# Sampled keys turned by VectorE in 32x32 squares instead of by TensorE, and their scores in four row groups

## What is computed

```python
past_k = cache_k[l][page_table].reshape(DB, past, N_HEADS, HEAD_DIM)   # DB = 8, past = 512
k_all  = jnp.concatenate([past_k, k], axis=1)
z      = jnp.einsum('bqhd,bkhd->bhqk', q, k_all) * (HEAD_DIM ** -0.5) + sb_bias
# sigmoids of -z are multiplied up from the last key to the first, their steps weight v_all
```

## Time and profile before

| | |
|---|---|
| median of 3 runs | 1088.38 us |
| profiled execution, its own time | 1088.52 us |
| its span, first to last instruction | 1086.7 us |
| TensorE busy | 1042.7 us (96%) |
| VectorE busy | 541.6 us (50%) |
| ScalarE busy | 308.5 us (28%) |
| mean granted TensorE clock | 0.986 of full speed |

### The profile page before, as it was taken

The page is one execution under the profiler, slowest core; times in us unless marked ns, Lnnn a source line. Parts: engine busy times, 40 slices in busy tenths (PEclk is TensorE's granted clock), DMA queues, the critical chain, the costliest instruction groups (busy, mean ns, idle before and its releaser), DMA issues.

```text
span 1086.7 us, 29226 instructions
## 1 busy us (share of the span) xinstructions
PE 1042.7 (96%) x12774; PEld 822.1 (76%) x12774; DVE 541.6 (50%) x1052; ACT 308.5 (28%) x592; POOL 176.2 (16%) x160
## 2 busy tenths in 40 slices
PE   7999999999999989999999999999999889989996
PEld 7999999966666549899876898656898556656565
DVE  6326654379875553344743554555445534343431
ACT  6323332266775552222411111111110110101011
POOL 1001300599300000100011111111111111111102
PEclk9999999999999999999999999999999998989998
DMA  7356785000106467767899999999999999999994
GB/s 246 108 166 202 228 277 152 1 14 2 40 27 214 149 233 263 235 227 274 319 368 385 384 387 386 387 381 375 385 377 388 377 392 397 382 388 395 381 390 110
DMA packets 85817, 293.19 MB, mean 270 GB/s; under 512 B 13426, under 2 KB 44850, under 8 KB 60070
## 3 DMA queue, kind: packets, MB, share of 16 engines
q1 hardware_dynamic: 78277, 273.30, 67.3%
q0 software_dynamic: 7280, 17.58, 6.8%
q10 hardware_dynamic: 128, 0.39, 0.1%
HBM read 272.98 MB, written 42.87 MB: 291 GB/s over the span
## 4 chain that ended last, share of the span: by engine, by line
PE 79%; DMA 13%; DVE 3%; SPq 2%; ACT 1%; issue 1%; POOL 0%; ACTq 0%; POOLq 0%
PE bank L2830 24%; PE bank L2375 12%; DMA w_all<-in_w_up 12%; PE bank L2612 8%; PE bank L2418 4%; PE bank L2847 4%; PE bank L2851 3%; PE bank L2584 3%; PE bank L2547 3%; PE bank L2456 2%; PE bank L2855 2%; SPq L1042 2%; PE bank L2479 1%; PE bank L2696 1%; DVE keep L1887 1%; PE bank L2371 1%
## 5 line engine op out<-in xcount | busy, mean ns | idle before, releaser
L2830 PE MATMUL bank<-w_all,xeT 128*32 128x256 f32 x6144 | 349.1, 385 | 19.2 <-DMA w_all<-in_w_up 15.6
L2830 PEld LDWEIGHTS bank<-w_all,xeT 128*32 128x32 f32 x6144 | 253.8, 111 | 107.4 <-issue 27.2
L2202 DVE STREAM_TRANSPOSE xeT<-xg 32x256 f32<-32x256 f32 x360 | 156.5, 435 | 102.7 <-DMA xg<-n_scr,tab 97.6
L2847 PE MATMUL bank<-w_all,hT 128*32 128x256 f32 x744 | 165.6, 379 | 0.0
L2851 PE MATMUL bank<-w_all,hT 128*32 128x512 f32 x744 | 129.0, 592 | 0.0
L1887 DVE TENSOR_TENSOR_SCAN keep<-keep,unseen 128x1024 f32<-128x1024 f32 (+7 forms) x64 | 94.8, 1514 | 37.2 <-ACT keep L1439 37.1
L2375 PE MATMUL bank<-w_hi,xh 128*128 128x256 f32 x376 | 108.1, 287 | 0.0
L2375 PE MATMUL bank<-w_hi,xl 128*128 128x256 f32 x376 | 105.5, 281 | 0.0
L2375 PE MATMUL bank<-w_lo,xh 128*128 128x256 f32 x376 | 105.5, 280 | 0.0
L2847 PEld LDWEIGHTS bank<-w_all,hT 128*32 128x32 f32 x744 | 81.8, 110 | 30.4
L1681 ACT ACTIVATE sgl<-bank 128x384 f32<-128x384 f32 x32 | 15.7, 491 | 304.0 <-PE bank L2830 304.0
(11 more groups left out here) (307 smaller groups left out, 1492.9 us busy)
## 6 DMA issues: line engine op xcount, KB each, us to landing
w_all<-in_w_down SPq DMA_DIRECT2D x64, 1024.0 KB, 30.0
w_all<-in_w_gate SPq DMA_DIRECT2D x64, 1024.0 KB, 29.4
w_all<-in_w_up SPq DMA_DIRECT2D x64, 1024.0 KB, 32.7
k_scr<-in_cache_k SPq DMA_DIRECT2D x32, 256.0 KB, 3.5
v_scr<-in_cache_v SPq DMA_DIRECT2D x32, 256.0 KB, 3.4
pgk<-k_scr SPq DMA_DIRECT2D x32, 256.0 KB, 4.0
w_raw<-in_w_in SPq DMA_DIRECT2D x7, 1024.0 KB, 7.1
pgv<-v_scr SPq DMA_DIRECT2D x4, 1024.0 KB, 5.9
```

Source lines behind the costliest of these rows:

```text
L2202: last = dve.transpose(xeT[i][rows_of(s), :, rows_of(g)], lane[:, :, s, :])
L2830: lasts = [pe.matmul(pair_ps(i)[rows_of(q), g, :, :], xeT[i][:, k, rows_of(g)], pair_of(b, i, k, q), start=(k == 0 and g != 1), stop=(k == ...
L2847: return pe.matmul(y_right_ps(g), hT[:, ft, rows_of(g)], w[ft // 2][:, ft % 2, DA:D], start=first and g != 1, stop=ends, skip_group_check= ...
```

## The change

`pgk` gets another layout: partition 32b + r holds row r of each of the 16 chunks (of 32 keys) of sequence b, so that one DMA fills 32 partitions. VectorE turns a set with four instructions of 128x512, in squares of 32x32, from SBUF to SBUF, two ahead of each of the two scans of the turn (`turn_keys`). After that, partition 32b + r of a chunk's square s holds column 32s + r of sequence b: the contraction over 128 columns lies in four slices of 32, all four of one sequence on the same 32 partitions. `past_scores` therefore has 16 matmuls for a set in place of 4: for each slice q, four matmuls with contraction over 32 partitions, sequence b in row group b and column group b. Their weights are windows of `qz_squares`, which VectorE clears and fills in turn 16 (`spread_squares`: one memset of 128x1056 and 16 copies), after the last pooling product, in whose place in SBUF it lies.

Gone are `past_keys` of TensorE and `copy_keys` of ScalarE and VectorE. SyncE waits for `s_hms` (keys turned) where it waited for `s_t`.

```diff
@@ places
+    SQUARE = PAGE // SQ
+    CHUNKS, SPLIT = PAST // SQUARE, P // SQUARE
+    pgk = [place(f"pgk{i}", [P, CHUNKS, P], F32, at_k[i])[0] for i in range(2)]
+    qz_squares, at = place("qz_squares", [P, HP * SPLIT * (DB // SQ) + 1, SQUARE], F32, at_m + 512 + 2 * slot)
@@ SyncE, load_keys(k)
-                    sp.wait_ge(s_t, turned("keys", k - 2, SQ - 1))
+                    sp.wait_ge(s_hms, keys_turned(k - 2))
                 for b in range(SQ):
-                    src = k_scr[SQ * g + b].rearrange("j p f -> p j f")[:, :, P * hp:P * hp + P]
-                    sp.dma_start(pgk[k % 2][:, b, :, :], src).then_inc(s_kld[k % 2], 16)
+                    src = k_scr[SQ * g + b].rearrange("j (c r) f -> r (j c) f", r=SQUARE)[:, :, P * hp:P * hp + P]
+                    sp.dma_start(pgk[k % 2][SQUARE * b:SQUARE * (b + 1), :, :], src).then_inc(s_kld[k % 2], 16)
@@ ScalarE and VectorE: copy_keys removed
@@ VectorE
+            def spread_squares():
+                dve.wait_ge(s_pm, NUS)
+                chain.link(dve.memset(qz_squares[:, :, :], 0.0))
+                out = qz_squares[:, 0:HP * SPLIT * NSG, :].rearrange("p (h s g) e -> p h s g e", s=SPLIT, g=NSG)
+                new = qT[:, :, TP:T].rearrange("p h (g b j) -> p h g b j", g=NSG, b=SQ)
+                for b in range(SQ):
+                    for q in range(SPLIT):
+                        last = dve.tensor_copy(out[SQUARE * b:SQUARE * (b + 1), :, q, :, SQUARE - DS:SQUARE],
+                                               new[SQUARE * q:SQUARE * (q + 1), :, :, b, :])
...
+            def turn_keys(k, half):
+                if half == 0:
+                    dve.wait_ge(s_kld[k % 2], 16 * SQ * (k // 2 + 1))
+                    dve.wait_ge(s_za, scored(NARROW_FROM - 1))
+                    dve.wait_ge(s_zb, scored(NARROW_FROM - 1))
+                    if k >= 2:
+                        dve.wait_ge(s_zp, SQ * (k - 1))
+                for q in range(2 * half, 2 * half + 2):
+                    last = dve.transpose(kTs[k % 2][:, q, :], pgk[k % 2][:, SPLIT * q:SPLIT * (q + 1), :].rearrange("p c f -> p (c f)"))
...
+                if i == NARROW_FROM - 1:
+                    spread_squares()
@@ TensorE: past_keys removed; past_scores(k)
-                for b in range(SQ):
-                    rows = slice(32 * b, 32 * b + 32)
-                    pe.matmul(z_past_ps[rows, :], qz[:, hp, SQ * g + b, :], kTs[k % 2][:, b, :],
-                              start=(hp == 0), stop=(hp == HP - 1)).then_inc(s_zp, 1)
+                keys = kTs[k % 2].rearrange("p q (c s r) -> p s q c r", s=SPLIT, r=SQUARE)
+                for q in range(SPLIT):
+                    n, h = (hp * SPLIT + q) * NSG + g, 2 * hp + q * SQUARE // HD
+                    lo = SQUARE * n + SQUARE - DS - DS * h
+                    for b in range(SQ):
+                        rows = slice(SQUARE * b, SQUARE * (b + 1))
+                        last = pe.matmul(z_past_ps[rows, :], qz_squares[rows, :, :].rearrange("p n e -> p (n e)")[:, lo:lo + SQUARE],
+                                         keys[rows, q], start=(hp == 0 and q == 0), stop=(hp == HP - 1 and q == SPLIT - 1))
+                        if q == SPLIT - 1:
+                            last.then_inc(s_zp, 1)
```

More of the change, by code:

```diff
@@ L454, in hybrid_step @@
     for i in range(NU + 2):
-        for k in range(NKEY):
-            if i == key_turn(k):
-                ring += [(("keys", k, j), "act" if j % 2 == 0 else "dve") for j in range(2)]
         for g in range(NSG):
@@ L462, in hybrid_step @@
                 ring += [(("smp", g), "dve")]
-        for k in range(NKEY):
-            if i == key_turn(k):
-                ring += [(("keys", k, j), "act" if j % 2 == 0 else "dve") for j in range(2, SQ)]
         if 1 <= i <= NU:
@@ L987, in _ @@
                 load_keys(k)
-            sp.wait_ge(s_t, turned("keys", NKEY - 2, SQ - 1))
+            sp.wait_ge(s_hms, keys_turned(NKEY - 2))
             load_values(2)
@@ L996, in _ @@
             load_values(5)
-            sp.wait_ge(s_t, turned("keys", NKEY - 1, SQ - 1))
+            sp.wait_ge(s_hms, keys_turned(NKEY - 1))
             def load_w_out(n):
@@ L1479, in keep_past @@
                                scale=-HD ** -0.5).then_inc(s_sgp, 1)
[L1481 to L1487, removed]
             def copy_sample_weights(g):
@@ L1572, in _ @@
                     keep_head(i, 0)
-                for k in range(NKEY):
-                    if i == key_turn(k):
-                        copy_keys(k, 0)
                 if i == 1:
@@ L1902, in sample_weights @@
                 dve.tensor_tensor(smp_w[:, :], smp_keep[:, 1:NKS + 1], smp_keep[:, 0:NKS], ALU.subtract).then_inc(s_am, 1)
-            def copy_keys(k, j):
-                n = ring_at["keys", k, j]
-                dve.wait_ge(s_t, turned("keys", k, j))
-                if k >= 2:
-                    dve.wait_ge(s_zp, SQ * (k - 1))
-                dve.tensor_copy(kTs[k % 2][:, j, :], bank[:, 4 + n % 2, :]).then_inc(s_td, 1)
+            def spread_squares():
[7 more added lines that the diff above has]
+                                               new[SQUARE * q:SQUARE * (q + 1), :, :, b, :])
+                        if (b, q) != (SQ - 1, SPLIT - 1):
+                            chain.done(last)
+                last.then_inc(s_qz, 1)
+            def turn_keys(k, half):
[7 more added lines that the diff above has]
+                    last = dve.transpose(kTs[k % 2][:, q, :], pgk[k % 2][:, SPLIT * q:SPLIT * (q + 1), :].rearrange("p c f -> p (c f)"))
+                    if q < CHUNKS // SPLIT - 1:
+                        chain.done(last)
+                if half == 1:
+                    last.then_inc(s_hms, 1)
             def lo_sample(g):
@@ L2470, in scores @@
                                 last.then_inc((s_za, s_zb)[a], 1)
-            def past_keys(k, samples):
-                if 0 in samples:
-                    pe.wait_ge(s_kld[k % 2], 16 * SQ * (k // 2 + 1))
-                for b in samples:
-                    n = ring_at["keys", k, b]
-                    free_bank(n)
-                    for j in range(NPG):
-                        last = pe.transpose(t_ps(n)[:, j, :], pgk[k % 2][:, b, j, :], ident[:, :])
-                    last.then_inc(s_t, 1)
             def new_scores(g):
@@ L2667, in _ @@
                     sum_values(i - 2, 0)
-                for k in range(NKEY):
-                    if i == key_turn(k):
-                        past_keys(k, (2, 3))
                 if 2 <= i < NU + 2:
```

22 lines of the change are left out of this document (10 added, 12 removed).

## The result

The changed kernel takes 1097.09 us, the median of four runs (1093.77 to 1099.6), where the kernel before took 1088.52 in four runs beside it: a ratio of 1.0076, 95% interval 1.0054 to 1.0098, which is 8.3 us more (5.9 to 10.7). Four more runs later gave 1.0083 (1.0066 to 1.0101). The forecast was 1093.2, so slower is right and 3.9 us are missing from the sum. The measured time lies above the forecast's own range (1090.8 to 1096) and inside the wide one (1088.8 to 1101.5).

A forecast was written before the change was run, and what follows sets the result against it. TensorE's issue was taken to bound the turns. Its own sum +2.6, recovered waits -1.1 and the start +3.3 gave +4.8 us on 1088.52: 1093.2 us, own range 1090.8 to 1096, wide range 1088.8 to 1101.5.

The forecast's parts named there:

- rival 2: Samples' scores: row groups side by side overlap only in part, 4.4 us a set, total 1099.8 us; 12%.
- TensorE's own sum: TensorE over eight sets: scores +20.5, page turns gone -16.7, sums merged -1.2, together +2.6 us.
- 3 (13.6): Samples' scores: one bank, one row group at a time, 13.6 us a set, total about 1174 us; 3%.
- rival 5: Samples' scores: the four groups of a set overlap in pairs, total 1079.6 us; 6%.
- waits of the ring: Turns 23 and 24: TensorE's waits for ScalarE's copies from the two-bank ring go, -1.1 us.
- rival 4: VectorE becomes the bound: a 128x512 turn takes 1.4 us instead of 0.72, total 1104 us; 4%.
- the DMA paragraph: Page loads: about 6 of 6.66 us needed, covered; a possible VectorE wait of about 1 us, mostly in spare time.
- The start: Turns 16 and 17: `spread_squares` delays VectorE's unit-16 scans and TensorE waits; together +3.3 us, between +0.5 and +4.5.
- the 0.5 for the first scores of the samples: After turn 17: VectorE's first key turns end at 335.6, TensorE wants them at 335.1, +0.5 us.
- Rival 1: The start is hidden, unit-16 scans hardly wait: 1090.5 us or less; 18%.
- That is +2.8 us: Turn 17: TensorE waits for both unit-16 scans and ends at about 333.0 instead of 330.2.
- What stays until the end: After attention: the weight stream moves by the same amount, so time gained or lost in the turns is kept.

The follow-up runs named there:

- the repeat: The changed kernel again, unaltered, against the kernel before: median 1097.6 us, ratio 1.0083; its profiled execution took 1093.79 us.
- e_warm: The changed kernel with eleven identity matmuls in turn 17 that keep TensorE from idling: 1092.6 us, ratio 1.0035.
- e_spread_in_before: The kernel before with `spread_squares` (one memset, sixteen copies) added in turn 16, read by nobody: 1092.28 us, ratio 1.0023.
- e_early_filled: The changed kernel with `qz_squares` filled in turns 11 to 15, plus eight identity matmuls in three later TensorE waits: 1090.63 us, ratio 1.0013.
- e_turned_scratch: The changed kernel with key pages laid in DRAM scratch in 32-column slices, scores again four matmuls over 128 partitions, no `qz_squares`: 1078.02 us, ratio 0.9901.
- the early squares: The changed kernel with `qz_squares` moved, cleared in turn 11 and filled in turns 12 to 15, run in two series: 1092.72 and 1093.28 us.
- e_before_filled: The kernel before with eight identity matmuls in its own waits at 392, 394 and 406 us: 1088.97 us, ratio 1.0004.
- e_one_group: The changed kernel with only the first of four contraction slices in the past keys' scores, 4 matmuls a set: 1086.48 us, ratio 0.9967.

## Why the prediction was right, and where it was short

The sign and the core of the sum are right by their mechanism. That the time lies in the stated range is partly luck: 1097.09 is above the forecast's own range of 1090.8 to 1096, and the part of the wide range that takes it in was there for rival 2 (1099.8), which the trace refutes.

*TensorE's own sum, +2.6, held.* A set's scores took 3.57 us (forecast 3.55), a turn 6.68 (forecast 6.66). Four tiles of 32x32 in four row and column groups, writing one bank, take (3.57 - 0.14) / 4 = 0.86 us, as much as the tail unit's tiles of 64 rows. With that rivals 2 (4.4 a set) and 3 (13.6) are out, and rival 5 (under 2.7) too. The Trainium skill's rule in "TensorEngine Tiling (Array Packing)", Restrictions and Gotchas, that different row tiles cannot access one bank at the same time, does not hold for this form: a single matmul of 512 columns takes 1.02 us in the trace before (`L2519`, 48 rows), so 16 one after another would take more than four times the 3.57 us that they do. The Trainium skill's 3.07 in "TensorE: Matmul & The Clock Gate", Part 3, gave an estimate of 1.11 us for a group; the trace gives 0.86.

*The waits of the ring, -1.1, went*: from 345 to 389 us the trace after shows none, TensorE being busy for all of it.

```profile
352.42:389.70 37.28, 37.28 (x336) 16.08 (x336) 25.85 (x38) 14.59 (x29) 0.00 (x0) 1.00 0.67 142
```

*VectorE's turn* takes 0.68 us by the groups of instructions, forecast 0.72, and the turns are hidden in every turn: rival 4 is out.

```profile
L1915 DVE STREAM_TRANSPOSE qT<-pgk 128x512 f32<-128x512 f32 x16 | 10.3, 679 | 1.2 <-DMA pgk<-k_scr 1.2
```

The pages' loads land in 4.8 us where they took 4.0. VectorE's one wait for a page, 1.2 us, lay inside its spare time, as the DMA paragraph allowed.

*The start: mechanism right, size short.* The spreading took 0.94 + 3.23 = 4.2 us (forecast 4.5), TensorE waited 1.92 + 0.75 = 2.7 (forecast 2.8), and the 0.5 for the first scores of the samples did not appear. Rival 1, a hidden start, is out. The step that failed is "That is +2.8 us": it priced the two waits by their length. Behind them the granted clock fell to 0.50 in the first profile, and turns 17 to 19 took 19.31 us (345.67 - 326.36) where the repeat needed 14.64 with the same waits: +4.7. With the clock held (repeat, and e_warm) attention costs +3.7 and +3.8, a little under the +4.8 of the sum. The profile before had no such stretch in turn 17, but it showed 0.986 as its mean clock and 0.97 from 816 to 1080 us, so that the clock falls somewhere was there to be read; I never put a term on it.

*What stays until the end, held.* From the first expert block to the end of the span it is 535.8 us before, 535.9 after and 535.7 in the repeat, and from the logits to that block 99.4 in all three. The variants scatter more: 534.5 to 537.1, and 96.7 to 100.8. So the last stages move a single execution by a us or two, whatever happens in attention.

*The output weights: not in the sum, and open.* From the output product to the logits it takes 43.4 us before, 45.6 and 45.0 in the two profiles of the changed kernel. There a part of `w_out` of 2 MB landed 10.3 and 9.8 us after its issue, 7.7 before, and ScalarE and VectorE, who split them, were late. In the chain after:

```profile
423.12 10.28 DMA wo_raw<-in_w_out
...
433.43 3.64 ACT wo_hi L1557
```

Of the variants some landed in 7.6 us (e_warm, e_spread_in_before) or 7.8 (e_early_filled, e_turned_scratch) and others in 9.7 and 10.1 (the two profiles of the early squares), so it doesn't follow from a part of the change. Where it landed in 7.6 to 7.8 us, that stage took 43.4 to 43.5 us; where in 9.7 to 10.3, 44.9 to 45.6 (e_before_filled fits less well: 7.9 and 44.4). Why it lands late no run tells. It would be worth 1.5 to 2 us of a run that has it.

The account by medians: +8.3 us for the change; e_warm, the clock of turn 17 given back, +3.7; the start moved away as well and the later waits filled, +2.0, where the sum without a start, 2.6 - 1.1, says +1.5. So of the loss some 4.6 us go with the idle TensorE of turn 17, most of it clock, 1.7 with the late start itself and the clock of the later waits together, and 2.0 are left, near what three more groups of scores cost beyond the turns of pages. These are differences of medians with intervals of up to 2 us either way, and the landing of the output weights is in each of them. One thing does not fit: the profiles price the late start at 2.7 us with the clock held (output product at 411.8 against 409.2), but the early squares, which have no late start, have no lower median than e_warm, which has it (1092.72 and 1093.28 against 1092.6). How the clock, the later waits and the weights share this out is open.

## What to carry to other kernels

Price a new wait on the busy engine twice: by its length, and by what the clock may cost behind it, here up to 5 us for 2.7 us of waiting, and go by a median of many runs, since a single profile shows one of the two outcomes. Where a table must be built by an engine that others wait for, build it turns earlier in its idle time, or keep TensorE occupied with matmuls into an unused bank. And when work is moved off the bound engine, count what the new layout makes that engine do instead: the page turns (2.2 us a set) were replaced by 2.6 us of narrower matmuls, while a layout changed already in DRAM kept the contraction full and won 10 us.

## What the runs showed of the hardware that was not expected

- The same two waits of TensorE (1.90 to 1.92 and 0.75 us) are followed by ten microseconds at 1.2 GHz in two executions (after, e_one_group) and by none in a third (the repeat). The waits of 0.63 and 0.95 us at 393 us were followed by about 7 us of it in one profile of the early squares and by none in the other. The Trainium skill, "TensorE: Matmul & The Clock Gate", Part 1, states that the clock has only these two levels and follows how busy the engine has been; the rows agree on the levels, and show that a wait's length alone doesn't settle it.
- The stretches at half clock were full of work, and their length differs: TensorE is busy for 1.00 of each microsecond from 332 to 341 before it gets its clock back, but only from 332 to 335 in e_spread_in_before.
- Four matmuls of 128x512 whose moving operand is read with 128 bytes between neighbours took 1.86 us for 0.99 with neighbours side by side. The Trainium skill, "SBUF — State Buffer", The DMA port swizzle, tells of lines of 16 bytes in SBUF and of a penalty for each access that goes to a new one; this trace agrees that such reading is slower, and its price here is 1.9 times.
- Tiles of 32 partitions cost per matmul what tiles of 64 and 128 cost: 0.86, 0.85 and 0.88 to 0.99 us for a group of four with 512 columns.
